# Moving the raw and rounded weight tiles by 32 bytes in SBUF, with their remainders left in place

## The reference, cut to what matters

```python
h = rmsnorm(x, norm_mix)
z = h @ w_in                          # (320, 2048) @ (2048, some 16,500), split among the mixers
...                                   # A: indexer, top-k attention; B: block attention; C: retention
m = sigmoid(g_a) * (o_a @ w_pa) + sigmoid(g_b) * (o_b @ w_pb) + sigmoid(g_c) * (o_c @ w_pc)
x = x + m @ w_out
h2 = rmsnorm(x, norm_ffn)
x = x + (gelu(causal_dwconv3(h2 @ ffn_up)) * (h2 @ ffn_gate)) @ ffn_down
```

## The kernel before, in words

| tile | offset before | modulo 64 | offset after | modulo 64 |
|---|---|---|---|---|
| epsc | 1024 | 0 | 35,776 | 0 |
| w_raw | 3040 | 32 | 3008 | 0 |
| w_hi | 19,424 | 32 | 19,392 | 0 |
| w_lo | 35,808 | 32 | 35,808 | 32 |
| h_hi, h_lo | 52,192, 72,672 | 32, 32 | as before | 32, 32 |
| m_hi, y_hi | 93,152 | 32 | as before | 32 |
| y_lo | 121,312 | 32 | as before | 32 |
| m_lo, oa_hi | 141,056 | 0 | as before | 0 |
| oa_lo, ob_hi, ob_lo | 151,296, 161,536, 171,776 | 0, 0, 0 | as before | 0, 0, 0 |

## Time and profile before

### The profile page before, as it was taken

How to read it: one execution, slowest core, us unless ns; L and a number is a source line. 1 busy time by engine, 2 the same in 40 slices (tenths; PEclk the granted TensorE clock), 3 DMA queues, 4 the chain that set the end, 5 groups by cost and what they waited for, 6 DMA issues and landing times.

```text
span 2427.4 us, 44519 instructions
## 1 busy us (share of the span) xinstructions
PE 2391.0 (99%) x17208; PEld 2293.7 (94%) x17208; DVE 1410.1 (58%) x2093; ACT 918.2 (38%) x1274; POOL 313.1 (13%) x626
## 2 busy tenths in 40 slices
PE   8999999999999999999999999999999999999997
PEld 7978999999999888888899999999999999999997
DVE  5545568899887544344445655656654346666443
ACT  5334343333433444334333344333333333333332
POOL 1135110000002222333200011000000000000001
PEclk9999999999999999999999999999999999999999
DMA  6447545556558888989676544444445544444553
GB/s 230 143 130 238 176 138 179 179 167 208 197 174 273 298 275 280 304 283 318 229 259 192 187 155 148 148 153 151 147 143 152 151 149 154 148 148 154 145 151 104
DMA packets 174386, 458.69 MB, mean 189 GB/s; under 512 B 24970, under 2 KB 74490, under 8 KB 174048
## 3 DMA queue, kind: packets, MB, share of 16 engines
q1 hardware_dynamic: 141040, 372.31, 47.1%
q0 software_dynamic: 26080, 75.67, 9.6%
q10 hardware_dynamic: 7056, 7.88, 0.9%
HBM read 425.27 MB, written 27.52 MB: 187 GB/s over the span
## 4 chain that ended last, share of the span: by engine, by line
PE 92%; DMA 2%; issue 2%; DVE 1%; ACT 1%; POOLq 1%; POOL 0%; DVEq 0%; SPq 0%; ACTq 0%
PE ps L778 85%; PE ps L1004 1%; DMA vpg<-in_cache_b_v 1%; PE ps L1045 1%; PE ps L851 1%; ACT w_hi L1086 1%; DMA vpg<-in_cache_a_v 1%; POOLq L675 0%; PE ps L1027 0%; PE ps L975 0%; DMA xT<-in_x 0%; PE ps L967 0%; PE ps L863 0%; POOL vpg L676 0%; PE ps L918 0%
## 5 line engine op out<-in xcount | busy, mean ns | idle before, releaser
L1333 DVE TENSOR_TENSOR w_lo<-w_raw,w_hi 128x1024 fp32r<-128x1024 f32 (+1 forms) x622 | 750.5, 1207 | 813.4 <-ACT w_hi L1086 808.5
L778 PE MATMUL ps<-h_hi,w_hi 128*128 128x320 f32 x3696 | 1161.2, 314 | 12.6 <-DVE w_lo L1333 11.5
L778 PE MATMUL ps<-h_hi,w_lo 128*128 128x320 f32 x3696 | 1142.8, 309 | 0.0
L778 PE MATMUL ps<-h_lo,w_hi 128*128 128x320 f32 x3696 | 1142.6, 309 | 0.0
L1086 ACT ACTIVATE w_hi<-w_raw 128x1024 fp32r<-128x1024 f32 (+1 forms) x622 | 647.5, 1042 | 817.7 <-PE ps L778 799.3
L778 PEld LDWEIGHTS ps<-h_hi,w_hi 128*128 128x128 f32 x3696 | 694.8, 188 | 51.6 <-issue 48.0
L778 PEld LDWEIGHTS ps<-h_lo,w_hi 128*128 128x128 f32 x3696 | 694.9, 188 | 0.7
L778 PEld LDWEIGHTS ps<-h_hi,w_lo 128*128 128x128 f32 x3696 | 694.4, 188 | 0.0
L778 PE MATMUL ps<-y_hi,w_hi 128*128 128x320 f32 x688 | 212.8, 309 | 1.5 <-DVE yt L1405 1.5
L778 PE MATMUL ps<-y_hi,w_lo 128*128 128x320 f32 x688 | 212.6, 309 | 0.0
L778 PE MATMUL ps<-y_lo,w_hi 128*128 128x320 f32 x688 | 212.6, 309 | 0.0
(11 more groups left out here) (320 smaller groups left out, 2019.6 us busy)
## 6 DMA issues: line engine op xcount, KB each, us to landing
w_raw<-in_w_in SPq DMA_DIRECT2D x258, 512.0 KB, 4.8
w_raw<-in_ffn_up SPq DMA_DIRECT2D x86, 512.0 KB, 3.8
w_raw<-in_ffn_gate SPq DMA_DIRECT2D x86, 512.0 KB, 3.6
w_raw<-in_ffn_down SPq DMA_DIRECT2D x80, 448.0 KB, 3.4
kpg<-in_cache_b_k SPq DMA_DIRECT2D x128, 128.0 KB, 4.2
vpg<-in_cache_b_v POOLq DMA_DIRECT2D x128, 128.0 KB, 4.8
kpg<-in_cache_a_k SPq DMA_DIRECT2D x128, 128.0 KB, 4.1
vpg<-in_cache_a_v POOLq DMA_DIRECT2D x128, 128.0 KB, 4.6
```

Source lines behind the costliest of these rows:

```text
L778: mm = mmul(bank[q][:, 0:T], wp[:, s, cols], xp[:, x.k0 + k, :], start=(x.first and k == 0 and t == 0), stop=(x.last and k == x.nk - 1 and ...
L1333: tt(w_lo[:, s, 0:n], w_raw[:, s, 0:n], w_hi[:, s, 0:n].bitcast(F32), ALU.subtract).then_inc(w_lo_done, 1)
```

## The change

`epsc`, a column of one float (32 bytes with its rounding), is allocated between `w_hi` and `w_lo`, not before the norm weights. Everything from `gmix` to `w_hi` begins 32 bytes sooner; `w_lo` and all behind it stay. No instruction, wait or transfer is added or taken away.

```diff
         ones = fix("ones", [P, P])
-        epsc = fix("epsc", [P, 1])
         gmix, gffn, gfin = fix("gmix", [P, KD]), fix("gffn", [P, KD]), fix("gfin", [P, KD])
         rstd = fix("rstd", [P, T])
         pt_sb = fix("pt_sb", [1, NB * NPG], I32)
         w_raw = fix("w_raw", [P, SLOTS, KU * P])
         w_hi = fix("w_hi", [P, SLOTS, KU * P], F32R)
+
+        epsc = fix("epsc", [P, 1])
         w_lo = fix("w_lo", [P, SLOTS, KU * P], F32R)
```

## The result

The changed kernel took 2411.57 us in the median of four runs (2411.2 to 2415.11), the kernel before 2428.76 us. The ratio is 0.9934, with a 95% interval of 0.992 to 0.9948: 17.2 us less. The forecast was 2403 us, with a range of 2394 to 2432.

What follows compares the result with a forecast made beforehand. TensorE's dense matmuls were taken to bound the kernel. From 2429.1 us, a gain of 29.7, less 1.7 in the output projection and 2.1 in the cache stretch, net 25.9, gave 2403 us, range 2394 to 2432.

Steps and rivals of the forecast that it cites:

- The bound and the lever: Dense matmuls at line 778 bound the kernel, 84.6% of the chain; operand addresses set their pace, 146.67 or 144.43 ns.
- Sign and stages: Stages change places: h, y, oa and ob gain 29.7 us together, the output projection m loses 1.7 us.
- 1,0,1 and 0,1,0: Per matmul of a set, moving tile and next weights differ in phase (1) or not (0); either pattern gains 2.24 ns per matmul.
- a phase modulo 64: A tile's start modulo 64 bytes; in dense matmuls only its change from one matmul to the next pays, 2.24 ns each.
- rival B: Alternating weights cost instead of paying, at the load of w_lo: 29.7 us more, 2459 us; chance 0.09.
- Something adds 13.3 ns: Each dense matmul takes 13.3 ns beyond its 320 columns' 133.3; line 792's plain fp32 matmuls supported two streams colliding.
- Rival A: In the dense matmuls only moving tiles' phases count, weights' do not: no change, 2429 us; chance 0.33.
- Rival C: Dense matmuls gain twice the 2.24 ns, as two weight tiles change phase per set: 2373 us; chance 0.03.
- Rival D: The paged-cache stretch takes back all its 4.3 us gain: 2405 us, inside the forecast; chance 0.55 together with the forecast.
- The cache stretch: From 780 to 1213 us, faster TensorE meets V pages earlier; half its 4.3 us gain counted, minus 2.1 us.
- VectorE, ScalarE, transfers, small tiles at nothing: Split, rounding, weight landing and small tiles cost nothing; split under 1 us at worst, landing 0 to 1 us in cache stretch.

Runs made afterwards that it cites:

- w_lo at phase 0 in the old order: Against the kernel before, w_raw and w_hi begin 64 bytes sooner and w_lo 32, tile order kept; 2403.3 and 2413.05 us, ratio 0.9921.
- every moving tile up: Against the kernel before, h, y and m_hi moved 32 bytes to oa's phase, epsc between w_hi and w_lo, gmix moved to qda's space; 2408.99 us, ratio 0.9921.
- h_lo alone: Against the kernel before, epsc placed between h_hi and h_lo, all weight tiles at one phase; 2415.79 us, ratio 0.9944.
- another order: The changed kernel with each set of three matmuls reordered to (w_hi, x_lo), (w_hi, x_hi), (w_lo, x_hi); 2413.71 us, ratio 0.9944.
- 128 bytes: Against the kernel before, gmix and gffn between w_hi and w_lo, so w_raw and w_hi begin 128 bytes sooner; 2408.75 us, one run.
- w_lo first: Against the kernel before, tiles ordered w_lo, w_raw, epsc, w_hi, activations unmoved; 2427.77 us, ratio 0.9996.
- half load: The kernel before, with all dense matmuls but a column block's first and last loading 64 of 128 weight columns; 2423.82 us, one run.
- the last kernel: Against the kernel before, every stage's w_hi lies two and w_lo one 32-byte step below both moving tiles, modulo 256; 2402.6 us, ratio 0.9896.
- 64 bytes: Against the kernel before, gmix between w_hi and w_lo, so w_raw and w_hi begin 64 bytes sooner; 2414.61 us, ratio 0.995.
- w_raw alone: Against the kernel before, epsc between w_raw and w_hi, so only w_raw and the small tiles move 32 bytes; 2428.28 us, ratio 1.0002.

## Why the prediction was right or wrong

**The bound and the lever: right.** TensorE's dense stream set the time, and the places of its operands moved its pace, by 1.5% at most between the paces that the forecast used (440.0 and 433.3 ns). That m was the one fast stage was the evidence, and it held: after the change m is the one slow stage.

**Sign and stages: right.** oa got all of m's rate and m lost it, both as forecast.

**The size in h and y: the term that was mis-sized.** "I take the gain, since 1,0,1 and 0,1,0 both alternate twice in a set" gave 2.24 ns per matmul; h and y gave (440.0 - 435.6) / 3 = 1.5. Put in its place: (13,250 - 768) x 1.47 = 18.4 us, plus oa and ob 768 x 2.2 = 1.7, minus m 1.7, is 18.4 us, where 17.2 were measured. Of the rest 0.8 us is ob, whose sets got quicker while its units did not.

**The reason: right in part, and its unit wrong.** "If the relation of the two streams that are read at once is what counts" is borne out as far as places go: h kept 433.3 ns when all its four tiles moved by 32 bytes (w_lo at phase 0 in the old order, against every moving tile up), moving either stream alone does change the pace (h_lo alone, w_hi alone), and another order changes m. That the two are read at once, and collide, was argued and not shown. But a phase modulo 64 with a 0 or a 1 is not that relation: 64 and 128 bytes matter too, w_lo first gave nothing in h where the same 0,1,0 had given all in m, and some arrangements are slower than 440.0 ns, which the prediction had only as rival B. And no rule of places alone can be right, since h took two paces in one kernel. That h gained at 32 bytes was, by this model, partly luck.

**"Something adds 13.3 ns", read from line 792 as the weight load's toll.** The half load did not halve it. The rows show that the surplus is there at the fast column rate and not at the slow one, and that it can shrink; what it is was argued, not shown. The eight matmuls of the earlier trace rows are also misread: the loop at line 792 has four, and the trace has two records for each, so 0.27 us is the distance of records and a plain fp32 matmul takes two of them. The comparison of records stands.

**Rival A** (moving tiles alone) fell: 17 us came from the weights' places. With the moving tiles untouched, h went from 440.0 to 435.6 ns per set because w_hi moved. With A falls the use that the prediction made of the Trainium skill's rule on the two read ports (TensorE: Matmul & The Clock Gate, Part 2), that the weights' place is idle: the trace doesn't agree with it. Whether the ports share anything, no run shows. **Rival B** did not occur in h, y and oa, but oa with 442.2 and 443.4 shows that moving the weights can cost as well; whether by B's mechanism is open. **Rival C** found no support; no stage was quicker than 433.3. **Rival D**, the forecast with the cache stretch taking its gain back, did not happen: that stretch gained.

**The cache stretch: half was taken off for nothing.** It gained 4.35 us with the changed kernel, more than its 768 sets at 4.4 ns (3.4 us). The risk that was argued is real, though: in the profiled executions of four quicker kernels (h_lo alone, w_lo at phase 0, 64 bytes, another order) waits of 1.7 to 2.5 us for a V page were followed by a half-rate clock, and one kernel's two runs lay 10 us apart. The change and the last kernel did not meet it in the executions profiled, though the change had a wait of 1.8 us too.

**VectorE, ScalarE, transfers, small tiles at nothing: right.** The split's mean stayed at 1224 ns, the landing at 4.9 us, and w_raw alone moved nothing.

## What to carry to other kernels

If matmuls of one shape run at different distances in different stages, with no wait in any, compare the operands' addresses before looking elsewhere: here 32 bytes, without one instruction changed, were worth 0.7%, and one good arrangement in all stages 1.0%. Don't reason from one pattern to the next; copy an arrangement that has been measured, for both parts of the moving tile and both of the weights, and measure it again in each stage, in more than one stretch of it, since one arrangement can have two paces. A quicker TensorE meets its slowest transfers sooner, and a wait there may cost about as much again in clock: 1.8 us of waiting, and 1.6 us in the unit behind it.

## What the runs showed of the hardware that had not been expected

- The distance between fp32r matmuls of 320 columns at 2.4 GHz took only a few values, from 433.3 to 443.4 ns per three in long stretches, held until the stream was interrupted or changed its tiles; the same tiles in the same places took 436.7 and 433.3 in one kernel, 433.3 and 440.0 in another, 435.6 and 440.0 in the changed one. Against 440.0 ns, 433.3 is 16 cycles of 2.4 GHz less in three matmuls, and 436.7 is 8.
- Halving the weight columns loaded beside a matmul shortened the load from 188 to 135 ns and left the pace of h and y at 440.0 ns per set.
- The granted clock fell to half for a few microseconds in the middle of a stream that was busy for 99% of the span, after a wait of 1.8 us for a V page (above). In the changed kernel's execution a wait of 1.8 us for a V page was followed by no such fall.
